# Two hybrid blocks on one core: latent attention with scores normalised block by block, its rotation split over three engines, and other steps for heads and gates

## The reference, cut to what matters

```
q = (rmsnorm(c_q, q_a_g) @ w_q_b).reshape(b, s, MLA_HEADS, MLA_QK_DIM)
q_nope = q[..., :MLA_NOPE_DIM]
q_rope = rope(q[..., MLA_NOPE_DIM:], cos[:, None, :], sin[:, None, :])
kv = (rmsnorm(c_kv, kv_a_g) @ w_kv_b).reshape(b, s, MLA_HEADS, MLA_NOPE_DIM + MLA_V_DIM)
...
    sc = (jnp.einsum('bqhd,bkhd->bhqk', qn, k_nope)
          + jnp.einsum('bqhd,bkd->bhqk', qr, k_r)).astype(jnp.float32) * scale
    mask = key_pos[None, :] <= q_pos[:, None]
    p = jax.nn.softmax(jnp.where(mask, sc, NEG), axis=-1)
    return jnp.einsum('bhqk,bkhd->bqhd', p.astype(v.dtype), v)
...
yb = mla_attention(...) * jax.nn.silu(gb)
x = x + jnp.concatenate([ya, yb], axis=-1) @ w_out[l]
```

## Time and profile before

| | |
|---|---|
| time, median of 3 runs | 2789.79 us (2789.72 to 2794.62) |
| the profiled execution's own time | 2790.87 us |
| its span, first to last instruction | 2789.1 us |
| PE busy | 2732.7 us (98%), 13100 matmuls |
| DVE busy | 1241.8 us (45%) |
| ACT busy | 1000.0 us (36%) |
| POOL busy | 1089.6 us (39%) |
| mean granted TensorE clock | 0.994 |
| PE busy in 400 to 540 us (latent stage, first layer) | 128.98 of 140.00 us |
| PE busy in 1100 to 1240 us (the same, second layer) | 128.05 of 140.00 us |

### The profile page before, as it was taken

The page is one execution under the profiler, slowest core; times in us unless marked ns, Lnnn a source line. Parts: engine busy times, 40 slices in busy tenths (PEclk is TensorE's granted clock), DMA queues, the critical chain, the costliest instruction groups (busy, mean ns, idle before and its releaser), DMA issues.

```text
span 2789.1 us, 33326 instructions
## 1 busy us (share of the span) xinstructions
PE 2732.7 (98%) x13100; PEld 2271.2 (81%) x13100; DVE 1241.8 (45%) x1831; ACT 1000.0 (36%) x1566; POOL 1089.6 (39%) x544
## 2 busy tenths in 40 slices
PE   8999998999999999899999999999999999999997
PEld 7888887888888888788878888888878888888886
DVE  6466636622346663672335545553443222222223
ACT  5244435523223443553433333332223323332222
POOL 1443332344443433334443333334344444444442
PEclk9999999999999999999999999999999999999998
DMA  6432231254443223124442232222223333336333
GB/s 183 132 84 76 73 121 45 66 142 143 123 132 91 69 76 121 45 67 138 138 120 76 76 83 76 73 80 80 87 83 121 113 109 111 114 113 211 117 125 113
DMA packets 307611, 289.13 MB, mean 104 GB/s; under 512 B 33152, under 2 KB 256000, under 8 KB 306944
## 3 DMA queue, kind: packets, MB, share of 16 engines
q1 hardware_dynamic: 300512, 264.40, 32.0%
q10 hardware_dynamic: 6944, 22.61, 2.1%
HBM read 260.19 MB, written 26.74 MB: 103 GB/s over the span
## 4 chain that ended last, share of the span: by engine, by line
PE 84%; DVE 11%; DMA 2%; ACT 1%; issue 1%; POOL 0%; SPq 0%; DVEq 0%; ACTq 0%
PE bank L873 25%; PE bank L875 24%; PE bank L874 24%; PE work L1131 1%; DMA w_raw<-in_w_in 1%; DVE pt L1728 1%; PE o_bank L874 1%; PE o_bank L875 1%; DVE mixed L1475 1%; PE work L987 1%; PE work L989 1%; PE o_bank L873 1%; DMA latent_scr<-mixed 1%; DVE probs L1680 1%; DVE mixed L1471 1%
## 5 line engine op out<-in xcount | busy, mean ns | idle before, releaser
L850 POOL TENSOR_TENSOR w_lo<-w_raw,w_hi 128x1024 fp32r<-128x1024 f32 (+3 forms) x460 | 982.0, 2137 | 1367.5 <-ACT w_hi L699 1367.5
L873 PE MATMUL bank<-act_in,w_hi 128*128 128x512 f32 x2662 | 1054.0, 396 | 12.8 <-DVE act_in L1443 9.9
L875 PE MATMUL bank<-act_in,w_lo 128*128 128x512 f32 x2662 | 1041.0, 391 | 0.0
L874 PE MATMUL bank<-act_in,w_hi 128*128 128x512 f32 x2662 | 1039.7, 391 | 0.0
L699 ACT ACTIVATE w_hi<-w_raw 128x1024 fp32r<-128x1024 f32 (+3 forms) x468 | 438.0, 937 | 1049.3 <-PE bank L875 648.4
L873 PEld LDWEIGHTS bank<-act_in,w_hi 128*128 128x128 f32 x2662 | 501.0, 188 | 116.8 <-DVE act_in L1443 11.2
L875 PEld LDWEIGHTS bank<-act_in,w_lo 128*128 128x128 f32 x2662 | 500.5, 188 | 107.2
L874 PEld LDWEIGHTS bank<-act_in,w_hi 128*128 128x128 f32 x2662 | 501.2, 188 | 98.9 <-issue 1.7
L873 PE MATMUL bank<-mixed,w_hi 128*128 128x512 f32 x768 | 299.7, 390 | 0.0
L875 PE MATMUL bank<-mixed,w_lo 128*128 128x512 f32 x768 | 299.1, 389 | 0.0
L874 PE MATMUL bank<-mixed,w_hi 128*128 128x512 f32 x768 | 299.0, 389 | 0.0
(11 more groups left out here) (267 smaller groups left out, 2703.7 us busy)
## 6 DMA issues: line engine op xcount, KB each, us to landing
w_raw<-in_w_in SPq DMA_DIRECT2D x512, 128.0 KB, 2.5
w_raw<-in_w_in SPq DMA_DIRECT2D x224, 256.0 KB, 2.9
w_raw<-in_w_out SPq DMA_DIRECT2D x64, 512.0 KB, 3.7
w_raw<-in_w_in SPq DMA_DIRECT2D x32, 512.0 KB, 3.7
w_raw<-in_w_out SPq DMA_DIRECT2D x64, 256.0 KB, 4.6
x_scr<-buf ACTq DMA_DIRECT2D x32, 256.0 KB, 3.2
probs<-x_scr SPq DMA_DIRECT2D x32, 256.0 KB, 5.0
w_raw<-in_w_attn_up SPq DMA_DIRECT2D x32, 256.0 KB, 2.9
```

The lines of the kernel that those rows point to most:

```text
L850: nc.gpsimd.tensor_tensor(lo, raw, hi, ALU.subtract).then_inc(lo_ready, 1)
L873: pe.matmul(dst, lhs[0], rhs[0], start=start, stop=False, skip_group_check=skip)
L874: pe.matmul(dst, lhs[0], rhs[1], start=False, stop=False, skip_group_check=skip)
L875: return pe.matmul(dst, lhs[1], rhs[0], start=False, stop=stop, skip_group_check=skip)
```

## The change

- **Tile order.** In `mla0` the rotated queries are now tile 0 (bank 0) and the plain queries tile 1.
- **Rotation.** DVE multiplies the rotated tile by cos as soon as the product is done; ACT's exchanged copies come after that; POOL multiplies them by sin, at the place in its order where ACT copies. Adding and splitting are a step of their own, `rotate`, 4 slots after the tile's last product in the first pair and 2 slots after in the others. A semaphore, `queries_rotated`, holds the even head's scores for it. PE waits for ACT's copies (`mla_hi`) before it overwrites bank 0 with tile 4.
- **Scores and norm.** `MLA_ORDER = ((3,), (2,), (1, 0))`: PE computes the block of 512 keys first, and maximum, scale, exponential, reciprocal and multiplication go in three rounds. After a latent head, scores start when two of the three `pt` parts are made, and only blocks 1 and 0 wait for the third.
- **Steps.** The odd heads' scores, norm and transpose stand one slot earlier (two products of a pair change place with them); those of heads 6 and 7 stand one slot later at transpose and values, and the output of head 7 too. The gate tiles' steps go from 4, 7, 9 / 11, 13, 15 / 22, 28, 30 / 32, 38, 40 to 1, 4, 6 / 16, 19, 21 / 24, 27, 29 / 32, 35, 37.

```diff
+MLA_ORDER = ((3,), (2,), (1, 0))
...
-            group("mla0", l, h // 2, [], ["qn", "qr both", "kn", "v both, half the tokens", "v, other half"],
+            group("mla0", l, h // 2, [], ["qr both", "qn", "kn", "v both, half the tokens", "v, other half"],
...
+                if kind == "mla0" and m == 0:
+                    later(4 if i == 0 else 2, "rotate", n)
+            lag = {3: 3, 4: 2}.get(m) if kind == "mla0" else None
-            lag = {1: 1, 3: 3, 4: 2}.get(m) if kind == "mla0" else None
...
-            head("mla", l, 2 * i, 0, [(1, "mla_scores"), (1, "mla_norm"), (4, "transpose"), (7, "values"),
-                                      (10, "output")])
+            head("mla", l, 2 * i, 0, [(1, "mla_scores"), (1, "mla_norm"), (4 if i < 3 else 5, "transpose"),
+                                      (7 if i < 3 else 8, "values"), (10, "output")])
...
-            head("mla", l, 2 * i + 1, 0, [(4, "mla_scores"), (4, "mla_norm"), (7, "transpose"),
-                                          (8 if i < 3 else 10, "values"), (12, "output")])
+            head("mla", l, 2 * i + 1, 0, [(3 if i < 3 else 4, "mla_scores"), (3 if i < 3 else 4, "mla_norm"),
+                                          (6 if i < 3 else 8, "transpose"), (8 if i < 3 else 11, "values"),
+                                          (12 if i < 3 else 13, "output")])
...
-                    at = ((4, 7, 9), (11, 13, 15), (22, 28, 30), (32, 38, 40))[k]
+                    at = ((1, 4, 6), (16, 19, 21), (24, 27, 29), (32, 35, 37))[k]
...
                     act.wait_ge(mm_done, tile_done[gi, m])
-                    if g["kind"] == "mla0" and m == 1:
+                    if g["kind"] == "mla0" and m == 0:
+                        act.wait_ge(bank_free, tile_no[gi, m] + 1)
...
+                    for blocks in MLA_ORDER:
+                        asked()
+                        for i in blocks:
...
+                        ins.then_inc(from_act, 1)
...
+                elif name == "hi" and groups[step[1]]["kind"] == "mla0" and step[2] == 0:
+                    g = groups[step[1]]
+                    swapped = probs2[:, T:2 * T]
+                    pool.wait_ge(mla_hi, swaps_before(step[1]) + 1)
+                    nc.gpsimd.tensor_tensor(swapped, swapped, sin[:, :], ALU.mult).then_inc(sin_done, 1)
...
+                if first and kind == "mla0" and m == 4:
+                    pe.wait_ge(mla_hi, swaps_before(gi) + 1)
...
-                    pe.wait_ge(pt_lo, h["turn0"])
+                    pe.wait_ge(pt_lo, h["turn0"] - after_mla(h))
...
+                        pe.wait_ge(queries_rotated, rotated_before(group_at["mla0", h["l"], h["h"] // 2]) + 1)
...
-                    for i in {"mla_scores": range(NB), "sb_scores": range(3), "sb_scores2": (3,)}[name]:
+                    for i in {"mla_scores": range(NB)[::-1], "sb_scores": range(3), "sb_scores2": (3,)}[name]:
...
+                        if i == 1 and after_mla(h):
+                            pe.wait_ge(pt_lo, h["turn0"])
...
+            def rotate_queries(gi):
+
+                c, swapped = probs2[:, 0:T], probs2[:, T:2 * T]
+                v.wait_ge(sin_done, rotated_before(gi) + 1)
+                link(v.tensor_tensor(c, c, swapped, ALU.add))
+                for e in range(2):
+                    ins = v.tensor_copy(qr_mla(e)[ROPE * e:ROPE * e + ROPE, :], c[ROPE * e:ROPE * e + ROPE, :])
+                link(ins)
...
+                ins.then_inc(queries_rotated, 1)
...
-                    answer()
-                    link(v.reciprocal(stat[:, 5, :], stat[:, 2, :]))
...
+                    for blocks in MLA_ORDER:
+                        answer()
+                        cols = slice(blocks[-1], blocks[0] + 1)
+                        link(v.reciprocal(stat[:, 5, cols], stat[:, 2, cols]))
```

More of the change, by code:

```diff
@@ L804, in _ @@
                 elif name == "mla_scores":
-                    asked()
-                    for i in range(NB):
-                        at, w = SCORE_AT["mla"][i], P * (i + 1)
-                        ins = act.activation(probs[:, at:at + w], score_bank("mla", i), ACT.Exp,
-                                             bias=stat[:, 1, i:i + 1], scale=MLA_SCALE,
-                                             accum_out=stat[:, 2, i:i + 1])
-                    ins.then_inc(from_act, 1)
+                    for blocks in MLA_ORDER:
+                        asked()
+                        for i in blocks:
+                            at, w = SCORE_AT["mla"][i], P * (i + 1)
+                            ins = act.activation(probs[:, at:at + w], score_bank("mla", i), ACT.Exp,
+                                                 bias=stat[:, 1, i:i + 1], scale=MLA_SCALE,
+                                                 accum_out=stat[:, 2, i:i + 1])
+                        ins.then_inc(from_act, 1)
                 elif name == "sb_scores2":
@@ L992, in meta_product, with after_mla @@
                 metas[0] += last
+            def after_mla(h):
+                return h["kind"] == "mla" and heads[h["j"] - 1]["kind"] == "mla"
             def y_before(g):
@@ L1425, in read_mla @@
                 his[0] += 1
-                v.wait_ge(mla_hi, his[0])
-                if g["kind"] == "mla0" and m == 1:
-                    c, swapped = probs2[:, 0:T], probs2[:, T:2 * T]
-                    v.tensor_tensor(c, src[:, :], cos[:, :], ALU.mult).then_inc(bank_free, 1)
+                if g["kind"] == "mla0" and m == 0:
+                    full(gi, m)
+                    v.tensor_tensor(probs2[:, 0:T], src[:, :], cos[:, :], ALU.mult).then_inc(bank_free, 1)
                     v.wait_ge(bank_free, tile_no[gi, m] + 1)
-                    rotate(swapped, c)
-                    for e in range(2):
-                        ins = v.tensor_copy(qr_mla(e)[ROPE * e:ROPE * e + ROPE, :], c[ROPE * e:ROPE * e + ROPE, :])
-                    link(ins)
-                    for e in range(2):
-                        own, other = slice(ROPE * e, ROPE * e + ROPE), slice(ROPE * (1 - e), ROPE * (1 - e) + ROPE)
-                        ins = v.tensor_tensor(qr_mla(e)[other, :], c[own, :], qr_mla(e)[own, :].bitcast(F32),
-                                              ALU.subtract)
-                    link(ins)
                 else:
+                    v.wait_ge(mla_hi, his[0])
                     v.tensor_tensor(dst[:, 1], src[:, :], dst[:, 0].bitcast(F32), ALU.subtract).then_inc(bank_free, 1)
@@ L1445, in read_mla @@
                 signal(tile_ready)
+            def rotate_queries(gi):
[5 more added lines that the diff above has]
+                link(ins)
+                for e in range(2):
+                    own, other = slice(ROPE * e, ROPE * e + ROPE), slice(ROPE * (1 - e), ROPE * (1 - e) + ROPE)
+                    ins = v.tensor_tensor(qr_mla(e)[other, :], c[own, :], qr_mla(e)[own, :].bitcast(F32),
+                                          ALU.subtract)
+                ins.then_inc(queries_rotated, 1)
             def read(gi, m):
@@ L1684, in _ @@
                     h = heads[step[1]]
[L1685 to L1695 removed]
+                    for n, blocks in enumerate(MLA_ORDER):
+                        v.wait_ge(scored, h["score0"] + n + 1)
+                        for i in blocks:
+                            ins = v.tensor_reduce(stat[:, 0, i:i + 1], score_bank("mla", i), AX_X, ALU.max)
+                        link(ins)
+                        cols = slice(blocks[-1], blocks[0] + 1)
+                        ask(v.tensor_scalar(stat[:, 1, cols], stat[:, 0, cols], -MLA_SCALE, None, ALU.mult))
+                elif name == "mla_norm":
+                    for blocks in MLA_ORDER:
+                        answer()
+                        cols = slice(blocks[-1], blocks[0] + 1)
+                        link(v.reciprocal(stat[:, 5, cols], stat[:, 2, cols]))
+                        for i in blocks:
+                            at, w = SCORE_AT["mla"][i], P * (i + 1)
+                            ins = v.tensor_scalar(probs[:, at:at + w], probs[:, at:at + w], stat[:, 5, i:i + 1], None,
+                                                  ALU.mult)
                     ins.then_inc(probs_ready, 1)
```

22 lines of the change are left out of this document (11 added, 11 removed).

## The result

| | kernel before | changed kernel |
|---|---|---|
| median of the runs, us | 2789.76 (2789.57 to 2794.62, 4 runs) | 2807.64 (2802.76 to 2807.89, 4 runs) |
| profiled execution, us; its span | 2790.87; 2789.1 | 2807.71; 2805.9 |
| granted clock over the span | 0.994 | 0.991 |
| stops of PE over 0.2 us in the latent stage, added up, first and second layer | 11.0, 11.0 | 16.2, 16.3 |

The changed kernel is slower: ratio 1.0056, 95% interval 1.0038 to 1.0073. I had forecast 2788 and a range up to 2798, so the result lies outside it. The ratio is that of the means, the table has medians. In the changed kernel the lines have moved: L873 is now L895, L1131 is L1162, L1443 is L1463, the last step of the rotation (L1439) L1477, L1694 is L1735, L1728 is L1769, `gate_mul` (L1566) L1602, and POOL's subtraction (L850) L867.

The account below looks back on a forecast made before the run. PE works nearly all the span, so only its stops, largely waits for DVE in the latent stages, could change. A layer: 3.7 - 2.9 + 1.2 - 0.3 - 0.5 = 1.2 us gained, two 2.4, less 0.5 for the clock: 2788, range 2779 to 2798.

Parts of the forecast that it names:

- To the first scores: Up to head 0's scores: one stop of 4 us becomes two of some 2.3 and 2.6; gain 0.2 at most.
- Head 0 to head 1: Head 0's scores to head 1's: transposes 0.4 us earlier, then about 3.2 us to the scores instead of 5.07, gain 1.2.
- DVE reads two value halves first as before: Before head 0's transposes: these readings stay ahead, so the transposes come only 0.4 us earlier than 5.39.
- Head 1 to head 2: End of head 1's scores to head 2's: 9.3 us instead of 10.53, transposes without a wait; gain 1.9.
- Head 2 to head 3: End of head 2's scores to head 3's: a new wait before head 3; a loss of 2.9 us taken.
- The two bounds: Before head 3's scores: `pt` parts ready at 10.7 us without contention from POOL, 12.3 with it; loss 2.1 or 3.7.
- the midway value: Before head 3's scores: a loss of 2.9 us, taken between 2.1 and 3.7 because two starts were too close.
- Head 3 to head 4: End of head 3's scores to head 4's: 9.9 us instead of 10.4, with one 0.68 product more; gain 1.2.
- Head 4 to head 5: End of head 4's scores to head 5's: 8.5 us if DVE is first, 10.1 if POOL; a loss of 0.3 taken.
- Head 5 to head 6: End of head 5's scores to head 6's: second `pt` part at 11.3 to 11.6 us; loss 0.5.
- The clock: PE's low clock level after stops: 0.5 us taken off the gain, for the new stop before head 3.
- Rival 3: Slower by the clock: low level at the start (2.8 us) and again before head 3 (2.3), 2798 us; chance 0.17.

Follow-up runs that it names:

- e1: The changed kernel with all gate tiles' steps back at those of the kernel before: 2789.58 us, ratio 0.9993.
- e9: The changed kernel with gate steps near the old, multiplications of tiles 0, 1, 3 behind the `pt` parts, one 768-column weight chunk held behind head 0's transposes: 2791.32 us.
- e3: The changed kernel with the first pair's rotation 2 slots after its product instead of 4: 2804.19 us, ratio 1.0045.
- e2: The kernel before with the new gate steps alone: 2812.79 us, ratio 1.0076.
- e15: The changed kernel with gate steps 4, 7, 9 / 11, 13, 17 / 22, 28, 30 / 32, 38, 43 and a 768-column chunk held behind head 0's transposes: 2780.48 us.
- e6: The changed kernel with the first gate tile alone at its old steps (4, 7, 9 instead of 1, 4, 6): 2799.94 us, ratio 1.0027.

## Why the prediction was wrong, step by step

- **To the first scores.** The first stop was forecast near 2.3 and is 2.50. The first product came at 431.77, 0.5 us ahead of the forecast, head 0's scores at 437.10, 0.65 behind the middle of it: between the two the chain took 1.2 us more. The rotation's steps L1471 and L1477 took 1.00 and 2.33 us for the 0.69 and 1.39 of undisturbed rows, with POOL's subtractions at 432.35 and 434.39 beside them. I had priced POOL's meetings only at `gate_mul`, and POOL's subtractions moved too. Nor is POOL's sin multiplication free, as the rows of head 5 below show.
- **Head 0 to head 1.** The transposes were to come 0.4 us earlier than 5.39 after the scores' end and came 1.3 later, 6.71. The failing step is "DVE reads two value halves first as before": `probs` was still multiplied behind them, but now while POOL subtracts 768 columns (2.15 us for 0.55). This term belongs to the new division and not to the gate steps: e1 has the same stop of 2.02 us. The rest of this stretch, 3.2, measured 3.21.
- **Head 1 to head 2.** Forecast 9.3, measured 9.39, and no wait at head 1's transposes: right.
- **Head 2 to head 3.** The two bounds were 10.7 and 12.3 us. Measured 12.17, POOL first by 0.06 us, in both layers. The order of the terms was right, the midway value wrong; the price of the meeting was right, 1.6 us forecast and 1.61 measured (2.30 less 0.69).
- **Head 3 to head 4** 9.4 for 9.9: a little better. **Head 4 to head 5** 10.4, again the upper of 8.5 and 10.1, POOL first by 0.02 us (0.20 in the second layer). **Head 5 to head 6** 11.75 for 11.6: right. Behind it the transposes of head 6 wait 0.42, which I had not.
- **The clock.** I took 0.5 us off for it; it cost 5.2, 7.0 at the two heads' scores less 1.8 ahead of them. Rival 3 had the mechanism, with both places, at a chance of 0.17, and priced them at 2.8 and 2.3 us; the first layer shows 1.9 and 2.6, the second 0.9 and 1.6. What spoke against it, that each new stop is shorter than 4.0 us, was wrong: it came behind some 3.4 us in each of the four kernels that have such a stop before head 3 without added work, behind 2.84 and 2.87 in both layers of e9, behind 2.02 before head 0's transposes in both layers of e3, and even behind 1.54 before head 4's scores in the first layer of e2 (these took 5.30 us at 0.68; in the second, behind the same stop, 3.73 at full speed).

The sin multiplication began 0.02 us ahead of the last scaling of head 5's maxima, which then took 1.29 us for 0.17. The exponentials, `probs` and the rotation stand behind it:

```profile
516.24 1.29 DVE L1727 TENSOR_SCALAR stat<-stat 128x2 f32<-128x2 f32 x1
```

```profile
516.22 1.29 POOL L879 TENSOR_TENSOR probs<-probs,sin 128x512 f32<-128x512 f32 x1 [1.79 <-ACT probs L802]
```

It is much the same in the second layer (1.26), in e1 and in e15. No run takes it away, so what PE would gain, at most 1.1 us a layer, is an estimate.

So the steps that failed were two. The sum took middle values at two meetings whose worse end came true both times, and didn't look for other meetings of the kind. And the clock was priced by whether one stop is as long as the one of before. The first layer closes by these terms: head 6's scores were forecast at 520.60 less 1.2, 519.4, and came at 527.14, 7.7 us later. Of that the first stretch gave 0.65, head 0's transposes 1.7, the way to head 3 0.7 and to head 5 1.0, to head 6 0.15, and the low clock in two heads' scores 4.5; to head 4 0.5 was gained. That is 8.2, and the 0.5 over is in the scores of heads 1, 2, 4 and 5, which took 3.56 to 3.67 us for 3.73.

The Trainium skill (SBUF — State Buffer, Who interferes with whom) says that a DVE instruction with two SBUF inputs, or one in a two-port mode such as `tensor_scalar` can enter, is blocked while a GpSimd operation that took the shared pair first runs. The trace agrees in the meetings shown here: `gate_mul` 2.30 and 2.25 us behind POOL's 768 columns, and `probs` 2.15. I had applied the page to `tensor_tensor` only; its line on `tensor_scalar` would have given the missed term. The `pt` parts and the bank readings, which have one of their two inputs in PSUM, took 1.62 and 0.69 us beside POOL as without it.

## What to carry to other kernels

Where two engines block each other, as DVE and POOL do here, and the plan has them start within 0.1 us of each other, don't take the middle: a few hundredths of a microsecond decide 1.6 us, either way round (e1 and e6). Take the order that is worse as the sum, look for it at every instruction of that kind in the stretch, and move one of them out of reach. A stop removed in front of one wait is only worth something if the chain behind it is shorter too; the order between two heads' work on DVE (rotation or `probs` first) decided that here. And a loss at several places is best split by undoing one entry of the table at a time: here the parts, 7.7 and 10.0 us, added up to the whole within what the runs can tell.

## What the chip showed that I had not expected

The same stops don't always bring the low clock. In e9 head 0's scores came behind the same two stops, 2.16 and 1.67 us, in both layers; the windows of these scores read

```profile
434.46:438.13 3.67, 3.67 (x24) 3.45 (x25) 2.13 (x5) 3.06 (x7) 0.85 (x1) 1.00 0.00 0
1134.63:1140.58 5.95, 5.95 (x24) 5.47 (x25) 2.13 (x5) 3.53 (x8) 1.28 (x1) 0.58 0.12 29
```

3.67 us at full speed and 5.95 at 0.58, so that one and the same plan has 2.3 us between its two layers. With the gate steps back (e1), where the same two places read 2.17 and 1.68 us in the first layer, the six passes between them ran at full speed there and at 0.52 in the second. What decides it at stops of this length stays open.
